# GpSimd's weight sums behind VectorE's input sums, a norm root ahead of a tile, and two input sums moved down, at the two edges of the mixer

## The chip, the cores and the metric

The kernel runs on one core of a Trainium2 chip, as one program. The metric is device time in microseconds (us). It was run three times without the profiler; the median was 3035.22 us (3034.07 to 3036.6). Every row below comes from one further, profiled execution.

## What is computed

The reference runs two transformer blocks over 512 tokens of width 1024, all in fp32. The first block has two layers of attention, a routed mixture of experts and a gated input. The second block is the one that matters here:

```python
f1 = swiglu(rms_norm(h, ffn1_pre_g), ffn1_w_gate, ffn1_w_up, ffn1_w_down)
h = h + 0.5 * rms_norm(f1, ffn1_post_g)
mix = hybrid_mixer(rms_norm(h, mix_pre_g), ...)
h = h + rms_norm(mix, mix_post_g)
f2 = swiglu(rms_norm(h, ffn2_pre_g), ffn2_w_gate, ffn2_w_up, ffn2_w_down)
h = h + 0.5 * rms_norm(f2, ffn2_post_g)
```

The change touches the two places where one of these three parts hands over to the next: ffn1 to the mixer ("the first edge") and the mixer to ffn2 ("the second edge"; in the code the first feed-forward part is `ffn(0)` and the last is `ffn(1)`).

## The kernel before, in words

**Layout.** The activations x lie transposed in SBUF as XT: 8 tiles of 128 partitions (1024 features) by 512 tokens. HT holds the same tiles times the gain of the next norm; the norm's factor (RSTD, one value per token) is multiplied in after the matmuls. Weights stream through a ring of six 1 MB slots; SyncE issues a load when TensorE has released the slot.

**Matmul units.** Most weight units are multiplied by a Strassen-like scheme of seven products instead of eight (`quartered_unit`, `multiply`, L1103): P1 and P2 use plain blocks, P3, P5, P6 and P7 use sums of weight blocks (S1 to S4, made by GpSimd in `weight_sums`, four additions at L3084, L3086, L3089 and L3092 for each unit, announced by wsum_ready), and P5, P6, P7 and P4 use sums of input blocks (T1 to T4, made by VectorE in `input_sums`, L2041, announced by t_ready). TensorE goes through the products in the order P1, P2, P3, P5, P6, P7, P4, and waits for wsum_ready ahead of P3 and for T1, T2, T3 and T4 ahead of P5, P6, P7 and P4. Weight sums alternate between two sets of buffers: GpSimd may begin a unit's sums only when the unit two before it is done on TensorE.

**An edge.** The last tiles of the part before become ready by halves of the tokens (256 columns each). For each half, ScalarE squares the last two tiles (`edge_squares`), TensorE sums the squares over the partitions (`half_norm`, L504 to L507), and ScalarE makes RSTD for that half from it (`half_root`: Ln at L2579, Exp at L2582). Then, for each of the eight tiles k, VectorE scales and adds to x (`residual_half`: L1424, then L1428), ScalarE writes HT (`raw_half`, L2590), and TensorE multiplies the tile by the first unit of the next part (`two_tiles_by_halves`, L516), which waits for every tile (raw_ready). TensorE's `half_norm` of half 1 stands behind tile 3 of half 0 in that loop. In between, ScalarE squares the new x (`x_square`, L2599) and VectorE adds the squares up (`add_x_square`, L1436) for the next norm; after half 1, eleven such additions remain.

All engines run their instructions in the order in which the program has them. The order around the edges is written out by hand. On ScalarE it is in `edge`: in the loop over half 0, raw tile k, then a square; after the loop the last square, then `half_root` of half 1, then the eight raw tiles of half 1, then their squares. On VectorE, `residual_by_halves` ends with the eleven additions and `raw_input_sums`, that is T1 to T4.

**After the first edge** TensorE finishes the first unit (L516), multiplies one more tile of the mixer's input (L1288, in bank 5 of PSUM) with the full norm sum in the middle of it (L489), and then goes on to three more plain tiles (L569), which need PSUM banks 0 and 1. VectorE, behind T1 to T4, copies two tiles (ROPEM, L2329), waits for the full RSTD (`rstd_wait`), and empties the first three PSUM tiles with `store_scaled` (L1499):

```python
v.tensor_copy(ROPEM, A3[:, 9:11, :])
rstd_wait()
store_scaled(CQ, 3, spare=2)
```

Its first two stores free the banks for which L569 waits. T1 to T4 of the mixer are first used after the three plain tiles.

**After the second edge** TensorE goes straight to the quartered unit 1 of ffn(1). Between its P3 and P5 stands the full norm sum (L489), which waits for the eleven additions.

**GpSimd** has, in its own order: the weight sums of ffn(0), then those of the first five mixer units (`weight_sums(at["mix"][0], ...)`), later the sums of three output units, of unit 1 of ffn(1), and then of units 2 and up of ffn(1). Unit 0 of ffn(1) has no sums.

Of the kernel before, what the change touches and what calls it, by code (L numbers as in the profile page):

```python
# [23 lines left out]
KD = D // P  # L24
# [193 lines left out]
def build_program(nc, A, out):  # L218
    with ExitStack() as ctx:
# [30 lines left out]
        CQ, CKV, KR, ROPEM = BIG[:, 0:3, :], BIG[:, 3:5, :], BIG[:, 5, :], BIG[:, 6:8, :]  # L250
# [26 lines left out]
        Q = {n: ctx.enter_context(nc.semaphore(n)) for n in names}  # L277
# [44 lines left out]
        at = {}  # L322
# [50 lines left out]
        def sum_tiles(a, h):  # L373
            return a[:, 0:h * NH].rearrange("p (k n) -> p k n", k=h)

        def input_blocks(src=HT):

            t = [GF[:, (4 + i) * D:(5 + i) * D] for i in range(4)]
            return ({"B11": src[:, 0:4, 0:NH], "B12": src[:, 0:4, NH:S], "B21": src[:, 4:8, 0:NH], "B22": src[:, 4:8, NH:S],
                     "T1": sum_tiles(t[0], 4), "T2": sum_tiles(t[1], 4), "T3": sum_tiles(t[2], 4),  # L380
                     "T4": sum_tiles(t[3], 4)})
# [23 lines left out]
        def token_half(half):  # L405
            return slice(NH * half, NH * (half + 1))
# [44 lines left out]
        def _(pe):  # L451
# [656 lines left out]
            def next_sums(n):  # L1108
                st["sums"] = st.get("sums", 0) + n
                return st["sums"] - n  # L1110
# [29 lines left out]
            def ffn(f):  # L1140
                t0, hid0 = next_sums(N_FFN_T), f * KF // 2
                u0, g0 = len(at["items"]), len(at["groups"])
                at[f"ffn{f}"] = (u0, g0)
                if f == 0:
                    drained("lin_ready")
                    drained("gate_ready")
# [78 lines left out]
                if f == 1:  # L1225
# [6 lines left out]
                    for k in range(OWN_X, KD):  # L1232
                        pe.wait_ge(Q["res_scaled"], now.next("res_scaled"))
                        b = k - OWN_X if k < OWN_X + 2 else 2 + k - OWN_X
# [4 lines left out]
            for L in range(LAYERS):  # L1239
                t0 = next_sums(4)  # L1240
# [60 lines left out]
            t0 = next_sums(4)  # L1301
# [39 lines left out]
            b = {}  # L1341
# [16 lines left out]
        def _(v):  # L1358
# [42 lines left out]
            def rstd_wait():  # L1401

                now.skip("gate_ready")
                now.skip("gate_free")
                v.wait_ge(Q["rstd_ready"], now.next("rstd_ready"))
# [25 lines left out]
            def add_x_square(n, half, k):  # L1431

                c, i = token_half(half), (2 * n + half) * KD + k
                v.wait_ge(Q["xsq_ready"], i + 1)
                v.wait_ge(*now.prev())
                v.tensor_tensor(ACC[:, c], XSQ[:, 0, :] if k == 1 else ACC[:, c], XSQ[:, i % 4, :], ALU.add)\  # L1436
                    .then_inc(Q["xsq_used"], now.inc("xsq_used"))

            def residual_by_halves(n, post, tiles, second):

                while st["summed"] < KD - 2:
                    sum_square()
                at["edge_x"] = at.get("edge_x", []) + [now.count("x_ready")]
                rstd_wait()
                for k in range(KD):
                    if k == tiles:
                        second()
                    residual_half(0, post, k)
                    if k > 4:
                        add_x_square(n, 0, k - 4)  # L1450
                rstd_wait()
                for k in range(KD):
                    residual_half(1, post, k)
                for k in range(4, KD):
                    add_x_square(n, 0, k)
                for k in range(1, KD):
                    add_x_square(n, 1, k)
                raw_input_sums(2 * KD)

            def norm(src, nt, gain, dst=None, name="h_ready", add=None, then_sum=False):  # L1460

# [29 lines left out]
            def store_scaled(dst, n, rows=P, scale=None, spare=None):  # L1491

                for k in range(n):
                    ps = lin_take()
                    if k == spare:
                        ps = PS[:, 5, :]
                    v.wait_ge(*now.prev())
                    if scale is None:
                        v.tensor_tensor(dst[0:rows, k, :], ps[0:rows, :], RSTD[0:rows, :], ALU.mult)\  # L1499
                            .then_inc(Q["lin_free"], now.inc("lin_free"))  # L1500
                    else:
                        v.scalar_tensor_tensor(out=dst[0:rows, k, :], in0=ps[0:rows, :], scalar=scale,
                                               in1=RSTD[0:rows, :], op0=ALU.mult, op1=ALU.mult)\
                            .then_inc(Q["lin_free"], now.inc("lin_free"))
# [529 lines left out]
                    v.tensor_tensor(XT[:, k, :], PS[:, k, :], XT[:, k, :], ALU.add)\  # L2034
                        .then_inc(Q["x_ready"], now.inc("x_ready"))

            def input_sums(b):

                for out, x, y in (("T1", "B12", "B11"), ("T2", "B22", "T1"), ("T3", "B22", "B12"), ("T4", "B21", "T2")):
                    v.wait_ge(*now.prev())  # L2040
                    v.tensor_tensor(b[out], b[x], b[y], ALU.subtract).then_inc(Q["t_ready"], now.inc("t_ready"))  # L2041

# [41 lines left out]
            def second_quarters(g, dst):  # L2084

                v.wait_ge(Q["unit_done"], at["groups"][g]["done"])
                quarter_add(U4, g, "P5", U2, "dve_step")
                quarter_add(dst[:, NH:S], g, "P3", U4, "tile_done")
                quarter_add(dst[:, S + NH:2 * S], g, "P5", U3, "tile_done")
# [18 lines left out]
                    v.scalar_tensor_tensor(out=a, in0=a, scalar=scale, in1=r, op0=ALU.mult, op1=ALU.mult)\  # L2108
                        .then_inc(Q[name], now.inc(name))

            def raw_input_sums(n=KD):

                v.wait_ge(Q["raw_ready"], now.next("raw_ready", n))
                input_sums(input_blocks())

            def ffn(f):
                g0 = at[f"ffn{f}"][1]
# [207 lines left out]
            g, last = at["ffn0"][1] + KF + 3, GF[:, 6 * S:8 * S]  # L2325
            first_quarters(g, last, 2)
            residual_by_halves(0, "ffn1_post", 5, lambda: second_quarters(g, last))
            v.wait_ge(*now.prev())
            v.tensor_copy(ROPEM, A3[:, 9:11, :]).then_inc(Q["dve_step"], now.inc("dve_step"))  # L2329
            rstd_wait()  # L2330
            store_scaled(CQ, 3, spare=2)
            store_scaled(CKV, 2)
            store_scaled(BIG[:, 5:6, :], 1)
            begin_sum("lin_free", QR // P + KVR // P + 1)
# [132 lines left out]
        def _(act):  # L2467
# [97 lines left out]
            def edge_squares(half, name, value, step):  # L2565

                c = token_half(half)
                act.wait_ge(Q["sq_used"], now.count("sq_ready"))
                for i in range(2):
                    act.wait_ge(Q[name], value + i * step)  # L2570
                    act.wait_ge(*now.prev())
                    act.activation(SQ[:, i, c], G[:, 6 + i, c], ACT.Square).then_inc(Q["edge_sq"], now.inc("edge_sq"))

            def half_root(half, bank):

                c = token_half(half)
                act.wait_ge(Q["gate_ready"], now.next("gate_ready"))
                act.wait_ge(*now.prev())
                act.activation(RSTD[:, c], PS[:, bank, c], ACT.Ln, bias=EPS_C[:, 0:1], scale=1.0 / D)\  # L2579
                    .then_inc(Q["gate_free"], now.inc("gate_free"))  # L2580
                act.wait_ge(*now.prev())
                act.activation(RSTD[:, c], RSTD[:, c], ACT.Exp, scale=-0.5)\  # L2582
                    .then_inc(Q["rstd_ready"], now.inc("rstd_ready"))

            def raw_half(half, k, name, base):

                c = token_half(half)
                act.wait_ge(Q["x_ready"], base + half * KD + k + 1)
                act.wait_ge(*now.prev())
                act.activation(HT[:, k, c], XT[:, k, c], ACT.Identity, scale=gain(name, k))\  # L2590
                    .then_inc(Q["raw_ready"], now.inc("raw_ready"))
# [10 lines left out]
            def edge(n, pre, banks, tiles, first, second):  # L2602

                del st["k"]
                edge_squares(0, *first)
                half_root(0, banks[0])
                for k in range(KD):
                    if k == tiles:
                        edge_squares(1, *second)
                    raw_half(0, k, pre, at["edge_x"][n])  # L2610
                    if k < 4:
                        x_square(n, 0, k)
                    elif k > 4:
                        x_square(n, 0, k - 1)
                x_square(n, 0, KD - 1)
                half_root(1, banks[1])
                for k in range(KD):
                    raw_half(1, k, pre, at["edge_x"][n])
                for k in range(KD):
                    x_square(n, 1, k)  # L2620
# [348 lines left out]
            for k in list(range(KD, 2 * KD)) + list(range(KD)):  # L2969
                b = GCOL["b_gate"] + k  # L2970
# [22 lines left out]
            for k in range(OWN_X, KD):  # L2993
                b = k - OWN_X if k < OWN_X + 2 else 2 + k - OWN_X
# [5 lines left out]
        def _(pool):  # L3000
# [95 lines left out]
            for L in range(LAYERS):  # L3096
# [30 lines left out]
                for q in range(NSEQ + 1):  # L3127
# [6 lines left out]
                    if q >= 2:  # L3134
                        pool.wait_ge(Q["y_ready"], y0 + q - 1)
                        scatter(q - 2)
                        kind, n = ORDER[q - 2]
# [3 lines left out]
            pool.wait_ge(Q["comb_ready"], LAYERS * TT)  # L3141
            u0 = at["ffn0"][0]
            weight_sums(u0, u0 + N_FFN_U, 0)
            weight_sums(at["mix"][0], at["mix"][0] + 5)
            pool.wait_ge(Q["unit_done"], at["mix_generic"])
            pool.dma_start(TOEP, A["c_lnc"]).then_inc(Q["toep_landed"], 16)
# [11 lines left out]
            weight_sums(at["out_mix"][0], at["out_mix"][0] + 3)  # L3158
            u0 = at["ffn1"][0]
            weight_sums(u0, u0 + 2, 1)  # L3160
            weight_sums(u0 + 2, u0 + N_FFN_U, 1)


# [145 lines left out]
```

## Time and profile before

| what | value |
|---|---|
| median of three runs | 3035.22 us |
| the profiled execution: time, span | 3036.14 us, 3034.4 us |
| TensorE matmul busy | 2950.5 us (97%) |
| VectorE, ScalarE, GpSimd busy | 1318.6, 652.9, 820.5 us |
| mean granted TensorE clock | 0.993 |

Lines such as L516 are lines of the kernel. PE is TensorE's matmul, PEld its weight loads (which run ahead of the matmuls and show best when it stood still), DVE is VectorE, ACT ScalarE, POOL GpSimd. An fp32 matmul shows as two records. "Idle before" in square brackets is how long the engine stood still ahead of the group, and what it waited for. PEclk 1.00 is 2.4 GHz, 0.50 is 1.2 GHz.

### The profile page before, as it was taken

What the parts mean: (1) busy time and instruction counts of PE and PEld (TensorE: products, weight loads), DVE (VectorE), ACT (ScalarE), POOL (GpSimd) and SP (SyncE); (2) the same over time, 40 slices, a digit from 0 to 9 for tenths busy, and PEclk for the clock granted to TensorE, in tenths of its full rate; (3) what the DMA queues carried; (4) which work ended last, traced back from release to release, by engine and by line L of the source; (5) the groups of instructions that cost most, each with busy time, mean ns of one, the idle gap of its engine ahead of it and who ended that gap; (6) DMA issues with size and microseconds to landing.
All of it is one profiled execution on the core that took longest, in us unless ns stands there. A gap on an engine that the chain in (4) does not pass through costs nothing.

```text
span 3034.4 us, 31785 instructions
## 1 busy us (share of the span) xinstructions
PE 2950.5 (97%) x12506; PEld 1887.6 (62%) x12506; DVE 1318.6 (43%) x2213; ACT 652.9 (22%) x1083; POOL 820.5 (27%) x625
## 2 busy tenths in 40 slices
PE   9999999999899999999998999999999999999998
PEld 7865464333478654643334688887664445788887
DVE  6734443111537335431225644434563464644442
ACT  2034413111210353131112300002112441300011
POOL 5400022222134000222221245443200102254442
PEclk9999999999999999999999999999999999999999
DMA  5211126999422111269995122221211201122220
GB/s 188 84 70 42 56 76 247 388 383 371 190 83 84 70 42 43 90 223 389 378 376 221 70 84 97 84 98 70 97 72 46 83 28 58 68 97 84 84 97 28
DMA packets 81379, 412.67 MB, mean 136 GB/s; under 512 B 25872, under 2 KB 26256, under 8 KB 34768
## 3 DMA queue, kind: packets, MB, share of 16 engines
q1 hardware_dynamic: 56608, 387.57, 33.5%
q0 software_dynamic: 24624, 23.08, 2.3%
q8 instruction: 99, 1.62, 0.2%
q14 instruction: 48, 0.39, 0.0%
HBM read 513.31 MB, written 31.46 MB: 180 GB/s over the span
## 4 chain that ended last, share of the span: by engine, by line
PE 90%; DVE 7%; ACT 1%; issue 1%; DMA 0%; DVEq 0%; POOL 0%; ACTq 0%; SPq 0%; POOLq 0%
PE PS L1103 37%; PE PS L1037 11%; PE PS L608 8%; PE PS L1059 5%; PE PS L594 5%; PE PS L686 4%; PE PS L569 4%; PE PS L1276 3%; PE PS L1011 1%; PE PS L840 1%; PE PS L781 1%; PE PS L528 1%; PE PS L895 1%; PE PS L904 1%; PE PS L1339 1%
## 5 line engine op out<-in xcount | busy, mean ns | idle before, releaser
L3084 POOL TENSOR_TENSOR ATT<-ring 128x512 f32<-128x512 f32 (+1 forms) x98 | 127.1, 1297 | 1221.8 <-PE PS L1103 741.6
L1103 PE MATMUL PS<-G,ATT 128*128 128x256 f32 x1360 | 323.8, 381 | 0.1
L1103 PE MATMUL PS<-HT,ring 128*128 128x256 f32 x1392 | 317.8, 379 | 3.8 <-ACT HT L2624 2.1
L1103 PE MATMUL PS<-G,ring 128*128 128x256 f32 x1232 | 291.5, 379 | 0.0
L1103 PEld LDWEIGHTS PS<-HT,ring 128*128 128x128 f32 x1392 | 264.1, 190 | 43.6 <-issue 3.5
L1103 PEld LDWEIGHTS PS<-G,ATT 128*128 128x128 f32 x1360 | 259.7, 191 | 38.0 <-issue 1.5
L608 PE MATMUL PS<-HT,ring 128*128 128x512 f32 x576 | 263.2, 600 | 0.0
L2806 ACT ACTIVATE TMP<-PS 128x256 f32<-128x256 f32 x92 | 35.4, 384 | 1056.9 <-PE PS L1103 939.7
L1103 PEld LDWEIGHTS PS<-G,ring 128*128 128x128 f32 x1232 | 234.3, 190 | 32.0
L1037 PE MATMUL PS<-ring,G 128*64 128x512 f32 x1024 | 226.8, 595 | 0.6 <-ACT G L2775 0.6
L608 PEld LDWEIGHTS PS<-HT,ring 128*128 128x128 f32 x576 | 104.5, 190 | 126.6 <-issue 120.2
L3092 POOL TENSOR_TENSOR ATT<-ring 128x512 f32<-128x512 f32 (+1 forms) x97 | 173.4, 1787 | 7.6
L1986 DVE TENSOR_TENSOR G<-PS,G 128x256 f32<-128x256 f32 x48 | 20.4, 425 | 319.6 <-ACT G L2781 319.3
L2057 DVE TENSOR_TENSOR BIG<-PS,TMP 128x256 f32<-128x256 f32 x100 | 42.4, 424 | 259.6 <-ACT TMP L2806 256.7
L1037 PEld LDWEIGHTS PS<-ring,G 128*64 128x64 f32 x1024 | 70.7, 137 | 134.0 <-issue 133.0
L1103 PE MATMUL PS<-HT,ATT 128*128 128x256 f32 x568 | 134.3, 379 | 0.0
L3086 POOL TENSOR_TENSOR ATT<-ring 128x512 f32<-128x512 f32 (+1 forms) x97 | 131.3, 1353 | 0.0
L3037 POOL DMA_INDIRECT expert_rows<-G,ATT x46 | 46.6, 1013 | 308.2 <-DVE G L1997 307.8
L3089 POOL TENSOR_TENSOR ring<-ATT,ring 128x512 f32<-128x512 f32 (+1 forms) x98 | 127.2, 1298 | 7.7
L1059 PE MATMUL PS<-ring,G 128*64 128x512 f32 x512 | 116.1, 595 | 9.5 <-DVE G L1979 6.0
L2057 DVE TENSOR_TENSOR G<-PS,TMP 128x256 f32<-128x256 f32 x40 | 17.0, 424 | 245.3 <-ACT TMP L2806 242.5
L2057 DVE TENSOR_TENSOR TMP<-PS,TMP 128x256 f32<-128x256 f32 x273 | 115.8, 424 | 10.6 <-PE PS L1103 1.3
(383 smaller groups left out, 4386.2 us busy)
## 6 DMA issues: line engine op xcount, KB each, us to landing
ring<-in_stream SPq DMA_DIRECT2D x163, 1024.0 KB, 4.8
ring<-in_experts_gu SPq DMA_DIRECT2D x128, 1024.0 KB, 8.9
ring<-in_experts_down SPq DMA_DIRECT2D x64, 1024.0 KB, 8.7
G<-expert_rows SPq DMA_DIRECT2D x8, 1024.0 KB, 7.5
h_tokens<-G POOLq DMA_DIRECT2D x2, 2048.0 KB, 7.6
XT<-in_xT SPq DMA_DIRECT2D x1, 1024.0 KB, 8.0
G<-in_pT POOLq DMA_DIRECT2D x2, 512.0 KB, 6.4
out_T<-XT SPq DMA_DIRECT2D x2, 512.0 KB, 3.7
```

What stands on the lines that cost most here:

```text
L569: mm = pe.matmul(ps[0:m, :], wv[:, k, c:c + m], rhs[:, k, :], start=k == 0, stop=k == nk - 1)
L594: mm = pe.matmul(ps, w[:, k, c:c + P], rhs[:, k, :], start=k == 0, stop=k == nk - 1)
L608: mm = pe.matmul(units["ps"], w[:, k, c:c + P], rhs[:, k, :], start=k == 0, stop=k == KD - 1)
L686: mm = pe.matmul(product(g, name), y[:, k, s * P:(s + 1) * P], x[:, k * 256:(k + 1) * 256], start=k == 0 and name in ("P1", "P2", "P3", "P ...
L1037: mm = pe.matmul(PS[r, 4 + q % 2, :], XGT[:, q % 2, k * P + CAP * side:k * P + CAP * (side + 1)], ws[side][:, kk * 512:(kk + 1) * 512], st ...
L1059: mm = pe.matmul(PS[r, n, :], HIDT[:, q % 2, j * P + CAP * side:j * P + CAP * (side + 1)], ws[side][:, j * D + n * 512:j * D + (n + 1) * 512],
L1103: mm = pe.matmul(product(g, name), x[:, k * P:(k + 1) * P], y[:, k, :], start=first and k == 0 and name in opening, stop=last and k == h - ...
L2057: v.tensor_tensor(out, product(g, x), y, ALU.add).then_inc(Q[name], now.inc(name))
L3084: pool.tensor_tensor(a["S1"], a["A21"], a["A22"], ALU.add)\
L3086: pool.tensor_tensor(a["S3"], a["A11"], a["A21"], ALU.subtract)\
L3089: pool.tensor_tensor(a["S2"], a["S1"], a["A11"], ALU.subtract)\
L3092: pool.tensor_tensor(a["S4"], a["A12"], a["S2"], ALU.subtract)\
```

## The change

Four edits:

1. GpSimd waits for all four input sums (t_ready) of the mixer before the weight sums of its first five units, and for all four input sums of ffn(1) before the weight sums of units 2 and up. (`at["ffn1"]` gets a third entry for it, the count of t_ready.)
2. In `edge`, at both edges, ScalarE runs `half_root` of half 1 ahead of raw tile 7 of half 0, instead of behind that tile and two squares.
3. At the first edge VectorE makes only T1 and T2 in `residual_by_halves`; T3 and T4 come behind `rstd_wait` and the three stores of CQ.
4. The copy of ROPEM comes behind T3 and T4, so behind the stores as well.

```diff
-                at[f"ffn{f}"] = (u0, g0)
+                at[f"ffn{f}"] = (u0, g0, t0)
@@ residual_by_halves
-                raw_input_sums(2 * KD)
+                raw_input_sums(2 * KD, slice(0, 4 if n else 2))
@@ input_sums, raw_input_sums: a part of the four sums
-                for out, x, y in (("T1", "B12", "B11"), ("T2", "B22", "T1"), ("T3", "B22", "B12"), ("T4", "B21", "T2")):
+                for out, x, y in (("T1", "B12", "B11"), ("T2", "B22", "T1"), ("T3", "B22", "B12"), ("T4", "B21", "T2"))[part]:
@@ VectorE, first edge
             residual_by_halves(0, "ffn1_post", 5, lambda: second_quarters(g, last))
+            rstd_wait()
+            store_scaled(CQ, 3, spare=2)
+            input_sums(input_blocks(), slice(2, 4))
             v.wait_ge(*now.prev())
             v.tensor_copy(ROPEM, A3[:, 9:11, :]).then_inc(Q["dve_step"], now.inc("dve_step"))
-            rstd_wait()
-            store_scaled(CQ, 3, spare=2)
             store_scaled(CKV, 2)
@@ ScalarE, edge
                 for k in range(KD):
                     if k == tiles:
                         edge_squares(1, *second)
+                    if k == KD - 1:
+                        half_root(1, banks[1])
                     raw_half(0, k, pre, at["edge_x"][n])
...
                 x_square(n, 0, KD - 1)
-                half_root(1, banks[1])
                 for k in range(KD):
                     raw_half(1, k, pre, at["edge_x"][n])
@@ GpSimd
             weight_sums(u0, u0 + N_FFN_U, 0)
+            pool.wait_ge(Q["t_ready"], at["mix"][2] + 4)
             weight_sums(at["mix"][0], at["mix"][0] + 5)
...
             weight_sums(u0, u0 + 2, 1)
+            pool.wait_ge(Q["t_ready"], at["ffn1"][2] + 4)
             weight_sums(u0 + 2, u0 + N_FFN_U, 1)
```

## Rows read from the trace of the kernel before

**Rows 1.** The page: busy time of TensorE over the span.

```profile
PE 2950.5 (97%) x12506; PEld 1887.6 (62%) x12506; DVE 1318.6 (43%) x2213; ACT 652.9 (22%) x1083; POOL 820.5 (27%) x625
```

**Rows 2.** TensorE's waits, 2095 to 2160 us: total, times, longest.

```profile
PE PS L516 <- ACT HT L2590: 5.6, 3, 3.1
PE PS L569 <- DVE BIG L1499: 2.4, 1, 2.4
```

**Rows 3.** TensorE's waits, 2600 to 2650 us, one of two.

```profile
PE PS L489 <- DVE ATT L1436: 1.9, 1, 1.9
```

**Rows 4.** TensorE's waits, 2640 to 3034 us, all of them.

```profile
PE PS L489 <- DVE ATT L1389: 1.7, 1, 1.7
```

**Rows 5.** TensorE's weight loads in order of time, first edge: start, us, [idle before].

```profile
2099.02 3.43 PEld L516 LDWEIGHTS PS<-HT,ring 128*128 128x128 f32 x16
...
2114.71 8.23 PEld L516 LDWEIGHTS PS<-HT,ring 128*128 128x128 f32 x32 [2.50 <-ACT HT L2590]
...
2122.97 0.41 PEld L1288 LDWEIGHTS PS<-HT,ring 128*128 128x128 f32 x2
...
2134.36 0.30 PEld L569 LDWEIGHTS PS<-HT,ring 128*128 128x128 f32 x2 [3.23 <-issue]
...
2157.71 3.32 PEld L1103 LDWEIGHTS PS<-HT,ring 128*128 128x128 f32 x16 [1.61 <-DVE BIG L1499]
```

**Rows 6.** By line, 2093 to 2160 us: duration in ns, min/median/max.

```profile
L1424 DVE SCALAR_TENSOR_TENSOR G<-G,GC,RSTD x16: 483/485/1394, 2094.3 to 2120.0; 128x256 f32<-128x256 f32 x16
...
L1428 DVE TENSOR_TENSOR XT<-XT,G x16: 424/425/1374, 2094.9 to 2120.6; 128x256 f32<-128x256 f32 x16
...
L1436 DVE TENSOR_TENSOR ATT<-ATT x14: 424/425/1349, 2101.9 to 2126.4; 128x256 f32<-128x256 f32 x14
...
L2590 ACT ACTIVATE HT<-XT,GC x16: 507/508/509, 2095.3 to 2121.0; 128x256 f32<-128x256 f32 x16
```

**Rows 7.** GpSimd in order of time: first and last of eight sums (first edge).

```profile
2101.66 1.27 POOL L3084 TENSOR_TENSOR ATT<-ring 128x512 f32<-128x512 f32 x1 [26.62 <-DMA ring<-in_stream]
...
2111.47 1.33 POOL L3092 TENSOR_TENSOR ATT<-ring 128x512 f32<-128x512 f32 x1
```

**Rows 8.** VectorE in order of time, first edge.

```profile
2100.81 0.48 DVE L1424 SCALAR_TENSOR_TENSOR G<-G,GC,RSTD 128x256 f32<-128x256 f32 x1
...
2121.08 5.72 DVE L1436 TENSOR_TENSOR ATT<-ATT 128x256 f32<-128x256 f32 x11
2126.90 1.23 DVE L2041 TENSOR_TENSOR G<-HT 128x1024 f32<-128x1024 f32 x1
...
2132.76 2.28 DVE L1499 TENSOR_TENSOR BIG<-PS,RSTD 128x512 f32<-128x512 f32 x3
2143.23 0.69 DVE L1499 TENSOR_TENSOR BIG<-PS,RSTD 128x512 f32<-128x512 f32 x1 [8.19 <-PE PS L569]
```

**Rows 9.** ScalarE, first edge: RSTD of half 1, and the full RSTD.

```profile
2112.72 0.42 ACT L2582 ACTIVATE RSTD<-RSTD 128x256 f32<-128x256 f32 x1
...
2130.12 0.63 ACT L2510 ACTIVATE RSTD<-RSTD 128x512 f32<-128x512 f32 x1
```

**Rows 10.** A window: busy us of each engine, PEclk, DMA share, GB/s.

```profile
2136.00:2138.00 2.00, 2.00 (x4) 0.88 (x3) 0.00 (x0) 0.00 (x0) 0.00 (x0) 0.50 0.03 12
```

**Rows 11.** The second edge in order of time, from four engines' timelines.

```profile
2615.69 8.46 PEld L516 LDWEIGHTS PS<-HT,ring 128*128 128x128 f32 x32 [2.42 <-ACT HT L2590]
...
2641.40 3.43 PEld L1103 LDWEIGHTS PS<-HT,ring 128*128 128x128 f32 x16
...
2611.58 0.51 ACT L2590 ACTIVATE HT<-XT,GC 128x256 f32<-128x256 f32 x1 [0.49 <-DVE XT L1428]
...
2614.15 0.48 DVE L1424 SCALAR_TENSOR_TENSOR G<-G,GC,RSTD 128x256 f32<-128x256 f32 x1 [2.08 <-ACT RSTD L2582]
...
2622.06 9.47 DVE L1436 TENSOR_TENSOR ATT<-ATT 128x256 f32<-128x256 f32 x11
...
2624.69 1.27 POOL L3084 TENSOR_TENSOR ATT<-ring 128x512 f32<-128x512 f32 x1 [29.78 <-PE PS L516]
```

More of the change, by code:

```diff
@@ L2035, in moe, with input_sums @@
                         .then_inc(Q["x_ready"], now.inc("x_ready"))
-            def input_sums(b):
-                for out, x, y in (("T1", "B12", "B11"), ("T2", "B22", "T1"), ("T3", "B22", "B12"), ("T4", "B21", "T2")):
+            def input_sums(b, part=slice(0, 4)):
+                for out, x, y in (("T1", "B12", "B11"), ("T2", "B22", "T1"), ("T3", "B22", "B12"), ("T4", "B21", "T2"))[part]:
                     v.wait_ge(*now.prev())
@@ L2109, in by_rstd, with raw_input_sums @@
                         .then_inc(Q[name], now.inc(name))
-            def raw_input_sums(n=KD):
+            def raw_input_sums(n=KD, part=slice(0, 4)):
                 v.wait_ge(Q["raw_ready"], now.next("raw_ready", n))
-                input_sums(input_blocks())
+                input_sums(input_blocks(), part)
             def ffn(f):
```

## The prediction

> **What bounds the kernel.** I read the page first: TensorE's matmuls are busy for 97% of the span [rows 1], so other engines matter only where TensorE stands still for them. The view of waits gives those places. At the first edge it waited 5.6 us for tiles of half 0 and half 1 and 2.4 us for a free PSUM bank [rows 2], at the second 1.9 us for the additions of squares [rows 3], and its weight loads stood 2.42 us for the first tile of half 1 [rows 11]. Behind 2640 us it waited 1.7 us in all, so what is won at either edge moves the end by as much [rows 4]; loads are issued when TensorE releases a slot, so they move too.
>
> The waits understate the loss; the order of weight loads shows it whole. One record of a 256-column matmul takes 0.2146 us (3.43 / 16), and one of 512 columns twice that, 0.429. The first edge's L516 has 64 records and three short sums between them (6 records): 70 x 0.2146 = 15.0 us. It ran from 2099.02 to 2122.97, which is 23.95 us: 8.9 lost [rows 5]. The next stretch, L1288 and its sums, took 2122.97 to 2131.13 (2134.36 less 3.23 idle), and the first load of L569 could have stood at 2131.38, one record's cycle behind the last; it stood at 2134.36: 3.0 lost. L569's 48 records should take 20.6 us; they took up to the last wait, 2157.71 - 1.61 + 0.43 = 2156.53, which is 22.2: some 1.6 to 1.7 lost without any wait. The clock shows why: at 2136 to 2138 it was granted at 0.50, 1.2 GHz, after TensorE had stood still [rows 10].
>
> **Why VectorE is late at the first edge.** By line, L1424, L1428 and L1436 take 0.485, 0.425 and 0.425 us in the median but 1.39, 1.37 and 1.35 at most [rows 6]. The long ones fall in the time in which GpSimd does the first two units' weight sums, 2101.66 to 2112.80, eight additions without a pause [rows 7]. These sums are wanted only at P3 of the mixer's first quartered unit, behind 2157.71 + 16 x 0.2146 = 2161.1 [rows 5]. So GpSimd's work, which is early by 48 us, makes VectorE's late. The second edge shows it again: eleven additions took 5.72 us at the first edge with GpSimd idle, and 9.47 at the second, where GpSimd began at 2624.69 in the midst of them [rows 8, 11].
>
> The Trainium skill (GPSIMD Engine Reference, section Specifications) says that GpSimd shares its SBUF interfaces with VectorE and that contention is with VectorE instructions of two SBUF inputs or in a two-port mode. The three slow lines have two SBUF inputs, so the trace agrees. By the same rule edit 4 puts the copy of ROPEM beside GpSimd's sums, where it may be slowed.
>
> **Edit 1 and 2, first edge.** Half 0, tile 5 starts on VectorE at 2100.81 [rows 8]. With GpSimd idle a tile takes 0.485 + 0.425 and two gaps of about 0.04, and with one addition 1.51. Tile 6 starts at 2102.32, tile 7 at 2103.83, and x of tile 7 is there at 2104.8. ScalarE finishes raw tile 6 at 2103.8 and its square at 2104.3; TensorE's sum of half 1 is done at about 2104.1; so the moved root runs from 2104.3 to 2105.25 and raw tile 7 to 2105.8. TensorE wants tile 7 at 2099.02 + 15.0 less 9 tiles of 0.858, which is 2106.3. So the root in front costs nothing here. Without the move, the root would follow tile 7 and two squares, none longer than a raw tile's 0.51, and end at 2107.2: the move is worth 2.0 us. RSTD of half 1 comes at 2105.25 instead of 2113.14 [rows 9]. From there VectorE paces half 1 at 0.98 us a tile against TensorE's 0.858: eight tiles end at 2113.1, raw tile 7 at 2113.7, and TensorE's last four records at 2114.6 (unhindered it would be 2114.0). Before it was 2122.97. **Gain 8.4 us**, of which 6.4 is edit 1 and 2.0 edit 2.
>
> **Edits 3 and 4.** The eleven additions (5.72 us) run from 2113.2 to 2118.9; TensorE wants their end at 2114.6 + 12 x 0.429 = 2119.7. T1 and T2 (1.23 each) end at 2121.5. The full RSTD came 7.78 us behind the first load of L1288 (2130.75 less 2122.97) [rows 5, 9], so now at 2122.35 (for this the sum of squares mustn't be late, and it isn't). Two stores take 1.45 (of 2.28 for three), and L569's first load followed 0.15 behind: 2123.95 [rows 8]. L1288 would release TensorE at 2114.56 + 8.41 (2131.38 less 2122.97) = 2122.97, so a wait of 1.0 us stays where 3.0 was. **Gain 2.0 us.** T3 and T4 now end at about 2127.1; they are wanted over 20 us later. The copy of ROPEM runs beside GpSimd; by the ratio of the slow rows (1.37 to 0.425) it may take 2 us more, but the next store waits for a plain tile until about 2131 (VectorE idled 8.19 us there) [rows 8]. Cost zero. With TensorE never idle for long, I take the clock to stay at 1.00: **1.7 us** of L569 come back. If it does fall, they don't. The wait for the last store, at 2157.71, stays. First edge: 8.4 + 2.0 + 1.7 = 12.1 us.
>
> **The second edge.** GpSimd was idle during half 0 and half 1 here, so only the root's move matters in L516. RSTD of half 1 came at 2614.12 [rows 11]. Raw tile 7 started at 2611.58, after 0.49 us of idling for VectorE, so ScalarE was free at 2611.1 [rows 11]. The root (0.95 with its gap) now ends at 2612.1, 2.0 earlier. Raw tile 7 moves behind it, to 2612.2, and ends at 2612.7, where TensorE wants it at 2612.4: 0.3 us lost. Two squares stand between it and half 1's first raw tile, 2614.3: TensorE, done at 2613.6, waits 0.7 there. VectorE then paces it: raw tile 7 of half 1 at 2620.5, the unit's end at 2621.4 instead of 2624.2 (2615.69 + 8.46). Gain 2.8, of which 0.8 is slow clock.
>
> Behind it, P1, P2 and P3 take 24 x 0.2146 = 5.15: 2626.5. The additions start at 2620.0 and, without GpSimd beside them, end at 2625.8, so the wait of 1.9 is gone. The sum of squares takes 0.86 (2627.4), and T1 is there at 2627.1, T2 to T4 at 1.25 each behind it, each ahead of its product of 1.72. The unit ends at 2627.4 + 32 x 0.2146 = 2634.25, against 2641.40 [rows 11]. **Gain 7.15 us.**
>
> What is late next: GpSimd's sums of unit 2 start only behind T4, at 2630.9. One unit's four additions take 5.57 us beside VectorE ((2112.80 - 2101.66) / 2) [rows 7], so they are done at 2636.5. P3 of unit 2 stands at 2634.25 + 3.43 = 2637.7. The margin is 1.2 us, and nothing is lost. Unit 3's sums follow and have some 7 us more. At the first edge the two units' sums run from 2127.1 to 2138.3, and P3 is wanted at about 2149.1: cover 11 us.
>
> **Sum.** 12.1 + 7.15 = 19.2 us. The profiled execution took 3036.14 us, so 3016.9; the runs' median was 3035.22, 0.9 below it, which gives 3016.0. I say 3016.5.
>
> **Rivals.**
>
> - *The clock falls still* (12%). At the first edge it fell behind waits of 2.5 and 3.2 us [rows 5]; the new ones are 1.0, and 0.3 and 0.7. Against it: a busy TensorE around them. If it falls at both edges, 1.7 and 0.8 are not won: 3019. The Trainium skill (TensorE: Matmul & The Clock Gate, part 1) has idling halve the clock too.
> - *GpSimd's sums of unit 2 come late* (12%). T4 might end later, or the four additions take 6 us or more. The price is what exceeds 1.2 us, at P3 only. If VectorE's multiplications by RSTD behind T4 stretch them by one half (2.8 us), 1.6 is lost: 3018. A second unit late as well gives 3021.
> - *Only the order pays, not GpSimd's wait* (5%). If the long VectorE instructions had another cause that stays, the moves win 2.0 + 2.0 + 2.0: 3029. That the long ones lie inside GpSimd's eleven us speaks against it.
> - *Slower* (3%). The wait behind T4 turns weight sums from early work into work on the path at the second edge. It decides against the change when unit 2's sums end over 1.2 + 19.2 = 20.4 us late, behind 2657; +25.5 us, as if three further units' sums stood in front and P3 waited for them, would give 3040. For it: the margin is just 1.2 us. Against: GpSimd has one unit to do there in 5.6 us and TensorE takes 12.0 for each, so a delay shrinks with each unit.
> - *No change* (3%): the time won is waited for later. The rows behind 2640 show nothing that has a time of its own [rows 4].
>
> **How the numbers follow.** The forecast has 65%. Its own range is 3014 (the residual 1.0, 0.5, 0.3 and 0.7 us vanish) to 3019. With the clock and GpSimd cases, 89% lie below 3023; some of that I give to terms mis-sized by a few us. The range 3013 to 3023 leaves out the order-only case, the slower one and no change. About 0.2%, 6 us, is what can be told from no change here; so faster 0.94 (the first three cases and the forecast), same 0.03, slower 0.03.
>
> **What the profile after would show.** No L1424, L1428 or L1436 over 0.5 us at the first edge. L516 to L1288's first load 15.5 us instead of 23.95. L569 begins some 1 us behind L1288, at a clock of 1.00. GpSimd starts right behind T4 at both edges. The eleven additions take 5.7 us at both. No wait at L489 at the second edge. A new wait at P3 of unit 2, a slow clock, or a raw tile 7 that TensorE waits for by more than 0.4 us would each prove a step wrong.

## The result, and the profile after

The changed kernel takes 3019.14 us in the median of four runs (3018.8 to 3020.51) against 3035.91 (3034.07 to 3040.99, four runs). The ratio is 0.9941, with a 95% interval of 0.9929 to 0.9953. The forecast was 3016.5, with 3013 to 3023 as its range and 0.94 for faster. A second comparison on another occasion gave 0.9941 again [0.9927, 0.9955].

The profiled executions took 3034.4 us (span) before and 3017.0 after: 17.4 us. The order of TensorE's weight loads shows where they went. First edge, start, length, engine, operation, and idle time before in brackets (kernel lines behind L2331 are one to four higher than before):

```profile
2100.84 3.43 PEld L516 LDWEIGHTS PS<-HT,ring 128*128 128x128 f32 x16
...
2109.43 5.05 PEld L516 LDWEIGHTS PS<-HT,ring 128*128 128x128 f32 x24 [0.41 <-ACT HT L2591]
...
2116.38 0.41 PEld L1288 LDWEIGHTS PS<-HT,ring 128*128 128x128 f32 x2
...
2125.79 0.30 PEld L569 LDWEIGHTS PS<-HT,ring 128*128 128x128 f32 x2 [1.24 <-issue]
...
2147.44 2.67 PEld L1103 LDWEIGHTS PS<-HT,ring 128*128 128x128 f32 x13 [1.61 <-DVE BIG L1499]
```

L516 to L1288 takes 15.54 us where it took 23.95, the next stretch 9.41 instead of 11.39, and L569 21.65 instead of 23.35: 46.60 in all instead of 58.69 [rows 5]. By line, 2095 to 2150 us, VectorE's instructions now all have one length (ns, min/median/max), where the longest had been three times the median [rows 6]:

```profile
L1424 DVE SCALAR_TENSOR_TENSOR G<-G,GC,RSTD x16: 483/485/485, 2096.2 to 2114.1; 128x256 f32<-128x256 f32 x16
L1428 DVE TENSOR_TENSOR XT<-XT,G x16: 424/425/426, 2096.7 to 2114.6; 128x256 f32<-128x256 f32 x16
L1436 DVE TENSOR_TENSOR ATT<-ATT x14: 424/425/427, 2103.7 to 2120.4; 128x256 f32<-128x256 f32 x14
```

TensorE's waits at the first edge are down to two, 2095 to 2160 us:

```profile
PE PS L1103 <- DVE BIG L1499: 0.8, 1, 0.8
PE PS L569 <- DVE BIG L1499: 0.4, 1, 0.4
```

The second edge, in order of time, from the timeline of all engines:

```profile
2593.73 2.56 PEld L516 LDWEIGHTS PS<-HT,ring 128*128 128x128 f32 x12
...
2602.51 0.73 PEld L516 LDWEIGHTS PS<-HT,ring 128*128 128x128 f32 x4 [0.35 <-ACT HT L2591]
...
2604.12 5.05 PEld L516 LDWEIGHTS PS<-HT,ring 128*128 128x128 f32 x24 [0.89 <-ACT HT L2591]
...
2609.84 5.72 DVE L1436 TENSOR_TENSOR ATT<-ATT 128x256 f32<-128x256 f32 x11
...
2611.09 3.43 PEld L1103 LDWEIGHTS PS<-HT,ring 128*128 128x128 f32 x16
...
2616.27 0.41 PEld L489 LDWEIGHTS PS<-ATT,MATS 128*128 128x128 f32 x2
...
2616.95 0.19 PEld L1103 LDWEIGHTS PS<-G,ATT 128*128 128x128 f32 x1 [0.27 <-DVE G L2041]
...
2620.75 1.28 POOL L3086 TENSOR_TENSOR ATT<-ring 128x512 f32<-128x512 f32 x1 [36.09 <-DVE G L2041]
...
2624.03 3.43 PEld L1103 LDWEIGHTS PS<-HT,ring 128*128 128x128 f32 x16
```

The eleven additions take 5.72 us instead of 9.47 [rows 11], there is no wait ahead of L489, and GpSimd starts 0.07 us behind T4. From L516 to unit 2 the edge takes 30.30 us instead of 37.42.

So the edges won 12.09 + 7.12 = 19.2 us. The stretch between them (446.3 us) and everything behind unit 2 are as long as before to 0.05 us. The missing 1.8 us lie ahead of the first edge, which this kernel reached at 2100.84 and the kernel before at 2099.02, in code that the change doesn't touch. Of these, 1.30 are there already at the first quartered unit of the kernel, whose first load stands at 21.32 us instead of 20.02: TensorE's first loads stand 0.86 us apart, which is half clock, until 11.0 us here and until 8.4 before.

### The profile page after: what moved, and what is told of

It reads as the page before. It is cut to its first block, busy times and chain, and to the rows that moved or that the text cites. A ratio compares the mean times of both kernels' runs of the same rounds, so it can differ in the third digit from the quotient of the medians.

```text
span 3017.0 us, 31787 instructions
## 1 busy us (share of the span) xinstructions
PE 2943.6 (98%) x12506; PEld 1884.5 (62%) x12506; DVE 1308.3 (43%) x2213; ACT 652.7 (22%) x1083; POOL 820.3 (27%) x625
## 4 chain that ended last, share of the span: by engine, by line
PE 67%; DVE 5%; ACT 1%; issue 1%; DMA 0%; DVEq 0%; POOL 0%; ACTq 0%
PE PS L1103 33%; PE PS L608 6%; PE PS L1037 5%; PE PS L1276 3%; PE PS L569 3%; PE PS L594 3%; PE PS L1059 3%; PE PS L686 2%; PE PS L840 1%; PE PS L895 1%; PE PS L516 1%; PE PS L1339 1%; PE PS L1011 1%; PE PS L1319 1%; PE PS L781 1%
## 5 line engine op out<-in xcount | busy, mean ns | idle before, releaser
L2057 DVE TENSOR_TENSOR BIG<-PS,TMP 128x256 f32<-128x256 f32 x100 | 42.4, 424 | 258.2 <-ACT TMP L2808 255.3
L2057 DVE TENSOR_TENSOR G<-PS,TMP 128x256 f32<-128x256 f32 x40 | 17.0, 424 | 245.3 <-ACT TMP L2808 242.5
L2057 DVE TENSOR_TENSOR TMP<-PS,TMP 128x256 f32<-128x256 f32 x273 | 115.8, 424 | 10.6 <-PE PS L1103 1.3
```

Of the source, the lines that this page charges most:

```text
L2057: v.tensor_tensor(out, product(g, x), y, ALU.add).then_inc(Q[name], now.inc(name))
```

## Experiments

All are read by the same stretches, from first weight load to first weight load, in us. "Between" is the mixer from its first quartered unit to the second edge's L516. Spans are of the profiled executions, one for each kernel.

| kernel | L516 starts at | L516 | L1288 | L569 | first edge | between | 2nd: L516 | unit 1 | second edge | span |
|---|---|---|---|---|---|---|---|---|---|---|
| before | 2099.0 | 23.95 | 11.39 | 23.35 | 58.69 | 446.3 | 20.20 | 17.22 | 37.42 | 3034.4 |
| all edits | 2100.8 | 15.54 | 9.41 | 21.65 | 46.60 | 446.3 | 17.36 | 12.95 | 30.30 | 3017.0 |
| wait_only | 2102.9 | 17.51 | 12.04 | 24.69 | 54.25 | 448.0 | 19.33 | 12.95 | 32.27 | 3030.5 |
| root_only | 2098.2 | 24.28 | 10.63 | 21.65 | 56.56 | 446.4 | 17.36 | 17.44 | 34.80 | 3028.9 |
| order_only | 2099.5 | 24.31 | 9.40 | 21.65 | 55.37 | 442.9 | 20.25 | 15.26 | 35.50 | 3026.4 |
| no_gpsimd_wait | 2100.1 | 24.00 | 9.41 | 21.65 | 55.06 | 448.0 | 17.36 | 16.18 | 33.54 | 3029.8 |
| wait_and_root | 2099.2 | 15.54 | 12.04 | 23.35 | 50.93 | 444.6 | 17.36 | 12.94 | 30.31 | 3018.1 |
| no_second_wait | 2100.2 | 15.55 | 9.41 | 21.65 | 46.60 | 446.3 | 17.35 | 16.18 | 33.54 | 3019.6 |
| held_until_unit1 | 2100.9 | 15.54 | 9.40 | 21.65 | 46.59 | 444.6 | 17.36 | 12.94 | 30.30 | 3018.4 |
| copy_first | 2103.8 | 15.54 | 9.52 | 21.65 | 46.72 | 443.0 | 17.35 | 12.95 | 30.30 | 3016.8 |
| tokens_first | 2100.0 | 15.54 | 9.41 | 21.65 | 46.60 | 446.3 | 17.36 | 12.95 | 30.31 | 3016.2 |
| all_edits_again | 2102.5 | 15.55 | 9.41 | 21.65 | 46.60 | 446.1 | 17.36 | 12.95 | 30.30 | 3018.6 |
| tokens_first_again | 2100.3 | 15.55 | 9.41 | 21.65 | 46.60 | 444.7 | 17.36 | 12.95 | 30.30 | 3014.9 |

Where an edge is undisturbed it repeats to 0.02 us; the columns outside it move by up to 5.6 us from one execution to the next. A single span therefore can't rank these kernels, and the edges can.

The column "between" can be counted out. A slow stretch shows in the windows of 2 us as a granted clock below 1.00, and each one in this column cost about 1.7 us. With none of them it is 442.9 to 443.0 (order_only, copy_first), with one 444.6 (wait_and_root, held_until_unit1), with two 446.1 to 446.4 (before, all edits twice, root_only, no_second_wait), with three 448.0 (wait_only, no_gpsimd_wait). The two profiles of tokens_first have three and two, and are about 1.6 below this series. None of the four edits shows in it.

### Each edit alone

**wait_only**, edit 1 in the kernel before:

```diff
+            pool.wait_ge(Q["t_ready"], at["mix"][2] + 4)
             weight_sums(at["mix"][0], at["mix"][0] + 5)
...
+            pool.wait_ge(Q["t_ready"], at["ffn1"][2] + 4)
             weight_sums(u0 + 2, u0 + N_FFN_U, 1)
```

> Edit 1 alone: GpSimd's two waits, ScalarE's and VectorE's order as before. Measured is each edge by itself, from the first weight load of L516 to the first load of the unit where the edge is over (first edge: the first quartered unit of the mixer; second: unit 2 of ffn(1)): before 58.69 and 37.42 us, with all edits 46.60 and 30.30. Theory (GpSimd's additions stretch VectorE's): no VectorE instruction of L1424, L1428 or L1436 over 0.5 us; half 1 still starts 2.0 us late for the late root and L569 3.0 us late for its bank, each with some slow clock behind it: first edge 52.2 to 53.0. Second edge: only the additions and the wait at L489 go, 33.1. Rival (the long instructions have another cause, the order pays): first edge 58.7, second 37.4.

L516 fell from 23.95 to 17.51 and the additions at the second edge no longer wait: unit 1 takes 12.95 instead of 17.22. By line, VectorE at the first edge:

```profile
L1424 DVE SCALAR_TENSOR_TENSOR G<-G,GC,RSTD x16: 484/485/485, 2098.2 to 2118.1; 128x256 f32<-128x256 f32 x16
```

No instruction is long any more, in VectorE's old order. The first edge as a whole, 54.25, missed the forecast of at most 53.0 by two terms. L569 lost 3.0 us to slow clock and not 1.7. And the stretch of L1288 grew to 12.04 from 11.39: VectorE begins its eleven additions (2119.19) just 1.24 us ahead of TensorE's first load of L1288 here and 1.89 us ahead before, so the bank for L569 comes 0.65 us later on TensorE's count. The second edge, 32.27, is below the forecast of 33.1; its L516, with the same waits as before, took 19.33 instead of 20.20 because the clock did not fall in it. The view of weight loads shows the load to load distance of one record at 0.86 us, twice 0.43:

```profile
2132.48 0.50 PEld L569 LDWEIGHTS PS<-HT,ring 128*128 128x128 f32 x2 [3.88 <-issue]
2133.49 0.34 PEld L569 LDWEIGHTS PS<-HT,ring 128*128 128x128 f32 x1 [0.52 <-issue]
2134.35 0.34 PEld L569 LDWEIGHTS PS<-HT,ring 128*128 128x128 f32 x1 [0.52 <-issue]
```

**root_only**, edit 2 in the kernel before:

```diff
+                    if k == KD - 1:
+                        half_root(1, banks[1])
                     raw_half(0, k, pre, at["edge_x"][n])
...
-                half_root(1, banks[1])
```

> Edit 2 alone: the root of half 1 ahead of raw tile 7. Theory: at the first edge the root is ready near 4 us earlier, but VectorE is still held up by GpSimd in tiles 5 to 7, so only 0.6 to 1.4 us are won: 57.3 to 58.1. Second edge: L516 ends 2.8 us earlier, and GpSimd's sums of unit 2 then fall on the additions as before: 34.7. Rival (the root's place is the main cause at the first edge): the first edge falls by 6 us or more, to under 53.

At the second edge L516 took 17.36, as with all edits. At the first it took 24.28, 0.3 more than before. The timeline tells why:

```profile
2106.98 0.42 ACT L2582 ACTIVATE RSTD<-RSTD 128x256 f32<-128x256 f32 x1
...
2109.67 1.30 DVE L1436 TENSOR_TENSOR ATT<-ATT 128x256 f32<-128x256 f32 x1
...
2111.08 1.30 DVE L1424 SCALAR_TENSOR_TENSOR G<-G,GC,RSTD 128x256 f32<-128x256 f32 x1
...
2113.43 9.00 PEld L516 LDWEIGHTS PS<-HT,ring 128*128 128x128 f32 x32 [2.54 <-ACT HT L2590]
```

The root was done at 2107.4, but VectorE, slowed by GpSimd, had half 0 in hand until 2111.0, and half 1 began with a long instruction. So the early root was hardly used, and TensorE's 32 records behind the wait took 9.00 us, more of them at the low clock, against 8.23 [rows 5]. The 2.1 us that this kernel won at the first edge are 1.7 of L569 at full clock and 0.8 in the stretch of L1288, less that 0.3. The expectation (0.6 to 1.4 won) holds neither for L516 nor for the edge. The rival, 6 us or more, falls. L569 stayed at full clock here behind 2.46 us of idle loads, with edits 3 and 4 absent, so its slow clock does not come with every long wait. The second edge took 34.80, as forecast (34.7).

**order_only**, edits 3 and 4 in the kernel before:

```diff
-                raw_input_sums(2 * KD)
+                raw_input_sums(2 * KD, slice(0, 4 if n else 2))
...
+            rstd_wait()
+            store_scaled(CQ, 3, spare=2)
+            input_sums(input_blocks(), slice(2, 4))
             v.tensor_copy(ROPEM, A3[:, 9:11, :])
-            rstd_wait()
-            store_scaled(CQ, 3, spare=2)
```

> Edits 3 and 4 alone: T3, T4 and the copy of ROPEM behind the three stores. Theory: the idle time of 3.0 us ahead of L569 falls to 1.0, and the 1.7 us of slow clock in L569 go with it: first edge 55.0. Rival (the clock falls for what TensorE did not do during L516, not for this wait): the 1.7 us stay, 56.7. Second edge 37.4 by both.

L1288 took 9.40 and L569 21.65: both as in the changed kernel, with L516 as slow as ever. The wait is 2.0 us shorter, and the slow clock in L569 is gone with it, though the clock had fallen during L516. The edge, 55.37, is near the theory's 55.0 and not the rival's 56.7, which no_gpsimd_wait repeats (L569 21.65 behind a slow L516). The second edge, which this kernel doesn't change, took 35.50 instead of 37.42: 1.7 less by clock in unit 1, and 0.3 less idle time ahead of L489.

**no_gpsimd_wait**, all edits but the first:

> All edits but the first: GpSimd's weight sums where they were. Theory: first edge 54.0 (0.6 to 1.4 won by the root, 3.7 by the order), second 34.7. Rival (GpSimd's wait does nothing): as with all edits, 46.6 and 30.3.

54.0 was expected at the first edge and 55.06 measured: the order gave its part, the root none. At the second edge 34.7 was expected and 33.54 measured, since the clock did not fall behind the wait at L489 (2.6 us) as it did in root_only behind the same wait. Put beside all edits (46.60 and 30.30), GpSimd's waits are worth 8.46 us at the first edge and 3.24 at the second on top of the others.

**wait_and_root**, edits 1 and 2:

> Edits 1 and 2 without 3 and 4: T1 to T4 and the copy ahead of the stores again. Theory: L516 as with all edits (15.54 us to L1288), then 3.0 us of idle time ahead of L569 instead of 1.0. If the clock falls for that wait, 1.7 more in L569: first edge 50.1. If it falls only when L516 was slow as well, 48.4. Second edge 30.30 by both.

50.93, against 50.1 with a fall of the clock and 48.4 without one; 0.65 of the miss is the bank's later coming, as in wait_only. On top of GpSimd's wait the root is worth 17.51 - 15.54 = 1.97, as forecast. Without edit 3, VectorE's bank comes 3.1 us late, and the clock falls behind this wait though L516 had run at full clock. Waits, and the window behind:

```profile
PE PS L569 <- DVE BIG L1499: 3.1, 1, 3.1
PE PS L1103 <- DVE BIG L1499: 0.8, 1, 0.8
```

```profile
2128.00:2130.00 2.00, 2.00 (x3) 0.68 (x2) 0.00 (x0) 0.00 (x0) 1.92 (x2) 0.50 0.00 0
```

Edits 3 and 4 are worth 12.04 - 9.41 = 2.6 us of waiting here, and 1.7 of clock. The clock's share is a matter of chance: without edit 3 L569 lost 1.7, 3.0, 1.7 and nothing (before, wait_only, wait_and_root, root_only), and with it nothing in all nine profiles.

### The waits' places

**no_second_wait**, all edits without the second of the two waits:

```diff
-            pool.wait_ge(Q["t_ready"], at["ffn1"][2] + 4)
```

> All edits, but GpSimd waits only at the first edge. Theory: first edge 46.6 as with all edits; at the second the additions run beside the sums of unit 2 again, up to 9.5 us instead of 5.7, TensorE waits over 2 us at L489, and the edge takes 34.7. Rival (the wait at the second edge only moves the sums and buys nothing): 30.3.

33.54 at the second edge. In order of time, GpSimd's first addition and VectorE's last seven, and TensorE's wait:

```profile
2610.93 1.39 POOL L3086 TENSOR_TENSOR ATT<-ring 128x512 f32<-128x512 f32 x1 [26.93 <-PE PS L516]
```

```profile
2611.29 7.13 DVE L1436 TENSOR_TENSOR ATT<-ATT 128x256 f32<-128x256 f32 x7
```

```profile
PE PS L489 <- DVE ATT L1436: 2.6, 1, 2.6
```

Seven additions took 7.13 us, which alone take 7 x 0.52 = 3.6. The collision is back behind L516, as before the change, with nothing else changed. The forecast of 34.7 counted slow clock as well, which this execution did not have.

**held_until_unit1**, GpSimd held longer at the second edge:

```diff
-            pool.wait_ge(Q["t_ready"], at["ffn1"][2] + 4)
+            pool.wait_ge(Q["unit_done"], at["items"][u0 + 1]["done"])
```

> All edits, but at the second edge GpSimd is held until unit 1 of ffn(1) is done on TensorE, 3.3 us longer than behind T4. This asks what margin the sums of unit 2 have. Theory: they end 5.5 to 6.1 us behind unit 1, P3 of unit 2 is wanted 3.45 us behind it, so TensorE waits 2.1 to 2.7 us there, and only there: from L516's first load to unit 3's first load 44.5 to 45.1 us, against 42.39 with all edits. Rival (each later unit's sums are late too, since they queue behind these): a wait at every unit, over 48 us and more behind it.

Waits, 2600 to 2700 us:

```profile
PE PS L1103 <- POOL ATT L3094: 2.7, 1, 2.7
```

Unit 2 took 15.08 us instead of 12.09, and from L516 to unit 3 it was 45.38; 44.5 to 45.1 was expected. The sums ended 6.5 us behind unit 1 (2622.41 to 2628.92) and not 5.5 to 6.1, since GpSimd began 0.46 us behind it. GpSimd's four additions took 6.05 us (2622.87 to 2628.92), the last of them beside VectorE. No later unit waited, so the rival falls. So the margin behind T4 is real but short: with all edits the sums ended at 2625.94, and P3 of unit 2 stood at 2624.03 + 3.46 = 2627.49, 1.55 us later.

**copy_first**, the copy of ROPEM between T2 and the wait for RSTD:

```diff
+            v.tensor_copy(ROPEM, A3[:, 9:11, :])
             rstd_wait()
             store_scaled(CQ, 3, spare=2)
             input_sums(input_blocks(), slice(2, 4))
-            v.tensor_copy(ROPEM, A3[:, 9:11, :])
```

> All edits but the fourth: the copy of ROPEM (0.69 us) between T2 and the wait for RSTD. With all edits VectorE idles 0.74 us there. Theory: the copy fits, the first edge stays at 46.6 within 0.1, so edit 4 buys nothing. Rival: the stores start later by the copy, 47.3.

46.72 against 46.60, not the rival's 47.3. The copy fits into VectorE's idle time ahead of RSTD but for 0.12 us; that is all that edit 4 buys. That this kernel has one of the shortest spans of the table comes from 443.0 us between the edges.

### One step further

**tokens_first**. The long instructions pointed to a third collision. Before and with all edits, GpSimd does the token unit's four additions of 1024 columns while VectorE turns the second pair of tiles, and TensorE waits 1.4 us at L686 for VectorE. GpSimd idles 21.6 us ahead of unit 3's sums, so the token unit's can go there:

```diff
             def sums_of(u):
-                return u + 1 - ("ffn1" in at and u > at["ffn1"][0])
+                m = u - at["mix"][0] if "mix" in at else 0
+                return u + 1 - ("ffn1" in at and u > at["ffn1"][0]) + {2: 1, 3: 1, 4: -2}.get(m, 0)
...
-            weight_sums(at["mix"][0], at["mix"][0] + 5)
+            m0 = at["mix"][0]
+            weight_sums(m0, m0 + 2)
+            weight_sums(m0 + 4, m0 + 5)
+            weight_sums(m0 + 2, m0 + 4)
```

> All edits, and on GpSimd the sums of the mixer's token unit (its fifth, four additions of 1024 columns) ahead of those of units 3 and 4, into the time in which GpSimd idles (2140 to 2161). Before and with all edits they run beside VectorE's rope of the second tile pair (three instructions of 3.3 us that take 1.23 alone), and TensorE then waits 1.4 us at L686 for VectorE. Theory: the ropes take 1.23 us, the wait of 1.4 us at L686 is gone, and the median falls by 1.4 us against all edits. Rival: the two weight tiles land too late (the last slot is free only near 2147), the sums run into those of unit 3, and the wait moves to a P3: no gain, or up to 2 us slower than with all edits.

> The changed kernel once more, for how far its times spread, beside the next one. What differs between executions outside the edges has been stretches of some four 512-column matmuls at half clock, 1.6 to 1.8 us each, behind waits of TensorE (near 461, 790, 1302, 1700, 2230, 2425 and 2507 us). Theory (chance): they come and go at the same places, the edges stay at 46.4 and 30.3, the median is 3018 to 3020. Rival (they depend on the code): each kernel has its own, always the same, and both its profiles agree in them.

> The token unit's weight sums ahead of those of units 3 and 4, once more. Its first profile had no wait at L686 (1.6 us won by 2199 us) and lost 1.6 us in a slow-clock stretch near 2230. Theory (chance): over many runs it is 1.4 to 1.6 us below the changed kernel of the same chip. Rival (the slow stretch comes with this order, since the wait ahead of it now falls otherwise): equal medians, and the stretch near 2230 is there again.

Kernel lines behind L634 are one higher here than with all edits. The wait at L686 is gone in both profiles of it. In the first, GpSimd's and VectorE's timelines:

```profile
2150.75 2.35 POOL L3087 TENSOR_TENSOR G<-ring 128x1024 f32<-128x1024 f32 x1 [11.55 <-DMA ring<-in_stream]
...
2157.91 2.35 POOL L3095 TENSOR_TENSOR G<-ring 128x1024 f32<-128x1024 f32 x1
2160.77 1.27 POOL L3087 TENSOR_TENSOR ATT<-ring 128x512 f32<-128x512 f32 x1 [0.50 <-PE PS L1104]
```

```profile
2179.20 1.23 DVE L1547 TENSOR_TENSOR G<-G,SIN 128x1024 f32<-128x1024 f32 x1
```

The sums end 0.5 us before unit 3's begin, and the instruction that takes 3.33 us with all edits takes 1.23. Read where L686 begins, TensorE has won 1.59 us. In the first profile it lost them again near 2230, behind a wait of 2.03 us that all these kernels have; the window of that execution, and the same stretch in order of time in the second profile:

```profile
2230.00:2232.00 2.00, 2.00 (x3) 0.67 (x2) 1.31 (x5) 1.12 (x3) 0.00 (x0) 0.50 0.00 0
```

```profile
2228.97 0.66 PE L841 MATMUL PS<-MATS,ATT 128*128 128x128 f32 x4 [2.04 <-DVE ATT L1732]
2229.46 3.60 PE L608 MATMUL PS<-HT,ring 128*128 128x512 f32 x8
```

In the second profile the eight records behind the same wait took 3.60 us, at full clock, where the first had 4.89; the stretch between the edges was 444.7, 1.6 less than with all edits. Three kernels without this order lost the same 1.7 us there (wait_only, no_gpsimd_wait, held_until_unit1), so it is chance and doesn't come with the order. all_edits_again bears this out: its edges are 46.60 and 30.30 again, but it has a slow stretch near 460 that the first profile of the changed kernel lacks, and lacks the one near 1300 that the first has. In the times the gain doesn't show: tokens_first had 3017.49 in the median of four runs (3013.84 to 3021.71) and 3019.73 of five (3016.68 to 3020.47), the changed kernel 3018.84 of five on the chip of the latter (3015.16 to 3021.05). So on one chip the median was 0.9 us higher, not 1.4 to 1.6 lower as forecast. The means over nine runs each are 3018.4 and 3018.8, with standard deviations of 2.4 and 1.9 us; the error of their difference is about 1.0 us, so the runs neither show a gain of 1.6 us nor rule it out. It is seen in the traces only.

## Why the prediction was right, and where it was off

- **The bound and the loss.** Right. 58.69 us at the first edge were to fall by 12.1 and fell by 12.09; the second by 7.15 and fell by 7.12. What was won moved the end in full: behind unit 2 nothing changed.
- **The cause.** Right, and shown: at the edges, long instructions of these three lines are there when GpSimd adds beside them (root_only, no_second_wait) and not when it is held (wait_only), whatever the order. The second rival, that the order pays and not the wait, falls.
- **Edit 1 and 2, first edge.** L516 was forecast at 15.5 and took 15.54. The split, 6.4 and 2.0, was measured as 23.95 - 17.51 = 6.44 and 1.97. That the 2.0 depends on edit 1 the prediction did not say: without it, at this edge, the root's place gave nothing in L516.
- **Edit 3.** Forecast: 3.0 us of idle time become 1.0. Loads stood 1.24 less the usual 0.25, which is 1.0. The 1.7 us of slow clock came back, as taken; that there were 1.7 to win was the chance of the profile before, since root_only lost none there. The prediction also read the clock as falling behind waits of 2.5 and 3.2 us at this edge. In the windows of the kernel before it was 1.00 up to 2110, then 0.72, and 0.50 from 2112: it fell at about the end of the 3.51 us of idle loads ahead of raw tile 7, before the wait of 2.50.

```profile
2108.00:2110.00 2.00, 0.00 (x0) 0.00 (x0) 1.97 (x2) 0.00 (x0) 1.98 (x2) 1.00 0.00 0
2110.00:2112.00 2.00, 1.14 (x3) 0.96 (x4) 1.57 (x2) 1.22 (x3) 1.86 (x2) 0.72 0.00 0
2112.00:2114.00 2.00, 0.93 (x3) 0.21 (x1) 0.79 (x2) 1.01 (x3) 0.80 (x1) 0.50 0.00 0
...
2110.86 1.35 PEld L516 LDWEIGHTS PS<-HT,ring 128*128 128x128 f32 x4 [3.51 <-ACT HT L2590]
```

- **Edit 4.** The copy was costed at up to 2 us more beside GpSimd, under cover. It took 0.69 as alone; GpSimd's addition beside it took 1.77 instead of 1.27. The cover was right and the price wrong. Moving it was needless but for 0.12 us.
- **Second edge.** Raw tile 7 made TensorE wait 0.35 (0.3 forecast), half 1's first tile 0.5 to 0.9 by matmuls and by loads (0.7), L516 took 17.36 (17.4). T1 cost nothing: unit 1 took 12.95, which is unit 2's 12.09 and 0.86 for the sum of squares. Slow clock was a larger part of the win than the prediction counted. Beside some 0.9 us in L516 (20.20 against wait_only's 19.33; 0.8 counted), unit 1 before held another 1.7 (17.22 against order_only's 15.26, less 0.3 of waiting). The sum has it all the same, because the new unit was built up from records at full clock; but the rival of a falling clock was priced too low for this edge.
- **The record's length.** The prediction divides 3.43 by 16 and leaves out the gap behind each group. From start to start it is 3.45 / 16 = 0.2156 us and not 0.2146 (2099.02 to 2102.47, 16 records), which is under 0.1 us in any of its terms.
- **What is late next.** T4 came 26.95 us behind L516's first load (26.9 forecast). The margin of 1.2 us was 1.55, since GpSimd's additions, now alone, took 5.19 and not 5.57.
- **The sum.** Forecast 3016.9 for the profiled execution's time, measured 3018.8. The step that was off is the silent one that all outside the edges keeps its time. It does so only on the average: the thirteen profiles reach the first edge between 2098.2 and 2103.8 us and take 442.9 to 448.0 between the edges. The 1.8 us of the profiled pair are within that. The median of the runs, 2.6 above the forecast, is well inside its range, and the range was needed for this, not for the uncertain terms.

## What to carry to other kernels

Read an instruction's minimum and maximum by line before its mean: a cluster at three times the median, in the very time in which another engine is at work, is a reason to ask whether that engine's work, if it is early, makes late what others wait for. Holding it back is the test and, here, the cure. Hold the early work back to the last moment at which its own reader is safe, and measure that margin (here 1.55 us). Where what is changed is a stretch of 50 us in 3000, compare the stretch between two fixed instructions of the trace: it repeats to 0.02 us where spans differ by several.

## What the runs showed of the hardware

- VectorE's additions and multiplications of two SBUF operands (256 columns) take 0.42 to 0.48 us alone and 1.30 to 1.50 beside GpSimd's additions, which take 1.26 to 1.46 there and 1.26 to 1.27 alone. The timelines of GpSimd and then of VectorE in root_only show that the two engines alternate, one instruction for one:

```profile
2102.19 1.46 POOL L3087 TENSOR_TENSOR ATT<-ring 128x512 f32<-128x512 f32 x1
2103.72 1.33 POOL L3090 TENSOR_TENSOR ring<-ATT,ring 128x512 f32<-128x512 f32 x1
2105.13 1.33 POOL L3093 TENSOR_TENSOR ATT<-ring 128x512 f32<-128x512 f32 x1
```

```profile
2102.55 1.38 DVE L1424 SCALAR_TENSOR_TENSOR G<-G,GC,RSTD 128x256 f32<-128x256 f32 x1
2103.96 1.37 DVE L1428 TENSOR_TENSOR XT<-XT,G 128x256 f32<-128x256 f32 x1
2105.43 1.30 DVE L1436 TENSOR_TENSOR ATT<-ATT 128x256 f32<-128x256 f32 x1
```

  So a short VectorE instruction costs here about the length of the GpSimd instruction beside it. With 1024 columns on both, VectorE's L1546 goes from 1.23 to 3.33 us and GpSimd's additions from 2.35 to 3.2 to 3.3 (the changed kernel, 2180 to 2189 us). The Trainium skill (SBUF — State Buffer, section SBUF: two separate sides) says that whichever of the two starts first holds the shared ports for its whole instruction and the other is blocked. The one-for-one order agrees; the lengths agree in part. Strictly in turn, a pair would take 1.27 + 0.42 = 1.69 us, and these take 1.44 (2102.55 to 2105.43 is two), so by these spans a part of each overlaps; with 1024 columns it would be 1.23 + 2.35 = 3.58 and is 3.36 (2180.07 to 2183.43).
- A copy of 1024 columns that VectorE began 0.05 us ahead of GpSimd's addition kept its 0.69 us, and the addition took 1.77. VectorE's adds from PSUM and SBUF (L2057, 0.42 us) were not slowed beside GpSimd (2624.86 to 2627.12 with all edits). In order of time, VectorE and GpSimd of the changed kernel:

```profile
2129.02 0.69 DVE L2332 COPY BIG<-ATT 128x1024 f32<-128x1024 f32 x1
2129.07 1.77 POOL L3086 TENSOR_TENSOR ATT<-ring 128x512 f32<-128x512 f32 x1 [52.21 <-DVE G L2041]
2130.79 1.26 POOL L3088 TENSOR_TENSOR ATT<-ring 128x512 f32<-128x512 f32 x1
```

- TensorE's clock falls to 1.2 GHz behind some waits and not behind others of the same length in the same code: behind the 2.0 us near 2230 in four of thirteen profiled executions, at 1.6 to 1.8 us a time. Such stretches come and go near 2230, 2425 and 2507 us, about 1.7 us each, and their number gives the length between the edges to 0.2 us. Ahead of the first edge they come and go too (near 460, 1300, 1630 and 1700 us), but what they cost there was not taken apart. Whether a wait of 3 us is paid once or half as much again is therefore part of its price: of the 12.1 us at the first edge, 1.7 were clock in L569.
